# A modulation product moved to plain f32 products on four column groups of TensorE, with its weights in a buffer of their own

## What is computed

```python
silu_c = jax.nn.silu(c)            # 1024 values, the latent stream
silu_cc = jax.nn.silu(c_ctx)       # 1024 values, the context stream
for i in range(DEPTH):             # DEPTH = 2
    m_lat = jnp.split(silu_c @ w_mod[i] + b_mod[i], 9, axis=-1)
    m_ctx = jnp.split(silu_cc @ w_mod[i] + b_mod[i], 9, axis=-1)

def moe_swiglu(h, router, wg, wu, wd):      # first block, second layer
    ...
    for e in range(8):
        out = out + combine[:, e:e + 1] * ((silu(t @ wg[e]) * (t @ wu[e])) @ wd[e])
```

## Time and profile before

| | |
|---|---|
| three executions, median (lowest to highest) | 3621.58 us (3621.06 to 3627.07) |
| the profiled execution | 3618.0 us, span on the core 3616.2 us |
| mean granted TensorE clock | 0.952 |
| TensorE busy with products | 3361.4 us, 93% |
| VectorE / ScalarE / GpSimd busy | 2069.9 / 1639.2 / 492.5 us |
| HBM read | 531.8 MB, 150 GB/s over the span |

### The profile page before, as it was taken

One profiled execution on the slowest core, in us unless ns is written; L12 is line 12 of the kernel. 1 busy time (PEld: TensorE's weight loads), 2 busy tenths in 40 slices (PEclk: granted clock), 3 DMA queues, 4 the chain that ended last, 5 costly groups with the idle time before them and its releaser, 6 DMA issues.

```text
span 3616.2 us, 60330 instructions
## 1 busy us (share of the span) xinstructions
PE 3361.4 (93%) x23090; PEld 3082.0 (85%) x23090; DVE 2069.9 (57%) x3212; ACT 1639.2 (45%) x2673; POOL 492.5 (14%) x558
## 2 busy tenths in 40 slices
PE   7889997779999999998999999989999999988898
PEld 7679997679999999998888897689888988975798
DVE  6855559546666667766333663566336733565554
ACT  4335443345665555655322454544224522344544
POOL 4400007400000000001000241233002400130000
PEclk9779998689999999999999999999999999988999
DMA  5313444326676666764232452134324422340253
GB/s 213 124 49 144 176 157 147 98 103 235 248 253 236 235 240 242 254 243 160 83 110 83 143 184 73 55 117 154 109 82 158 173 101 94 121 152 1 94 186 106
DMA packets 99259, 536.72 MB, mean 148 GB/s; under 512 B 16162, under 2 KB 28002, under 8 KB 51339
## 3 DMA queue, kind: packets, MB, share of 16 engines
q1 hardware_dynamic: 93840, 522.05, 40.8%
q0 software_dynamic: 3200, 9.41, 1.0%
q10 hardware_dynamic: 1978, 1.75, 0.2%
HBM read 531.79 MB, written 10.74 MB: 150 GB/s over the span
## 4 chain that ended last, share of the span: by engine, by line
PE 84%; DVE 9%; ACT 4%; issue 2%; POOL 1%; DMA 0%; ACTq 0%; SPq 0%; DVEq 0%; POOLq 0%
PE PS L966 24%; PE PS L968 23%; PE PS L967 23%; PE PS L1006 4%; PE PS L1133 3%; DVE WL L1597 3%; DVE CONV L1782 3%; PE PS L1112 2%; PE PS L1122 1%; ACT WH L1271 1%; PE PS L1087 1%; POOL TMP L887 1%; DVE RSTD L1614 0%; PE PS L1152 0%; DVE TMP L1916 0%
## 5 line engine op out<-in xcount | busy, mean ns | idle before, releaser
L1597 DVE TENSOR_TENSOR WL<-RAW,WH 128x1024 fp32r<-128x1024 f32 (+2 forms) x1080 | 1228.1, 1142 | 819.0 <-ACT WH L1271 810.9
L966 PE MATMUL PS<-UH,WH 128*128 128x256 f32 (+2 forms) x4672 | 1437.8, 308 | 109.1 <-DVE H L1929 27.1
L1271 ACT ACTIVATE WH<-RAW 128x1024 fp32r<-128x1024 f32 (+2 forms) x1080 | 1049.5, 974 | 960.9 <-PE PS L968 919.7
L967 PE MATMUL PS<-UL,WH 128*128 128x256 f32 (+2 forms) x4672 | 1435.7, 307 | 0.0
L968 PE MATMUL PS<-UH,WL 128*128 128x256 f32 (+2 forms) x4672 | 1433.4, 307 | 0.0
L966 PEld LDWEIGHTS PS<-UH,WH 128*128 128x128 f32 x4672 | 898.6, 192 | 158.1 <-issue 110.7
L968 PEld LDWEIGHTS PS<-UH,WL 128*128 128x128 f32 x4672 | 899.3, 192 | 36.8
L967 PEld LDWEIGHTS PS<-UL,WH 128*128 128x128 f32 x4672 | 896.4, 192 | 38.3
L966 PE MATMUL PS<-HIDH,WH 128*128 128x256 f32 (+2 forms) x1848 | 546.3, 296 | 0.0
L968 PE MATMUL PS<-HIDH,WL 128*128 128x256 f32 (+2 forms) x1848 | 545.2, 295 | 0.0
L967 PE MATMUL PS<-HIDL,WH 128*128 128x256 f32 (+2 forms) x1848 | 545.1, 295 | 0.0
(11 more groups left out here) (184 smaller groups left out, 3030.7 us busy)
## 6 DMA issues: line engine op xcount, KB each, us to landing
RAW<-in_w_gu SPq DMA_DIRECT2D x214, 1024.0 KB, 4.8
RAW<-in_w_dn SPq DMA_DIRECT2D x168, 704.0 KB, 4.1
RAW<-in_w_mod SPq DMA_DIRECT2D x72, 1024.0 KB, 4.9
RAW<-in_w_in SPq DMA_DIRECT2D x30, 1024.0 KB, 5.0
RAW<-in_w_na SPq DMA_DIRECT2D x20, 1024.0 KB, 4.8
RAW<-in_w_o SPq DMA_DIRECT2D x12, 1024.0 KB, 4.8
RAW<-in_w_proj SPq DMA_DIRECT2D x8, 1024.0 KB, 4.8
RAW<-in_w_out SPq DMA_DIRECT2D x8, 1024.0 KB, 4.8
```

Source lines behind the costliest of these rows:

```text
L966: pe.matmul(ps, wh, mh, start=opens and x == 0, stop=False)
L967: pe.matmul(ps, wh, ml, start=False, stop=False)
L1271: act.activation(WH[slot][:, 0:hi - lo], RAW[:, s % RAW_SLOTS, lo:hi], ACT.Copy).then_inc(s_hi, 1)
L1597: dve.tensor_tensor(WL[slot][:, 0:hi - lo], RAW[:, s % RAW_SLOTS, lo:hi], WH[slot][:, 0:hi - lo].bitcast(F32), ALU.subtract).then_inc(s_lo, 1)
```

## The change

- The modulation steps leave the phase "moe": its body now has 19 steps (11 + 8), all evacuated by DVE. `RAW`, `WH` and `WL` see no modulation tile any more, and `SC4` and the work that made it are gone.
- POOL, in a loop of its own, loads each tile of `w_mod` in two halves of 0.5 MB into `MRAW[:, b, :]` (two halves, one transfer each, 144 in all). The transfer for a half is issued when PE has finished the half two before it (`s_mpc`).
- PE does one half after each of the first 18 steps of an expert (`mod_half`): four plain f32 products, with the two conditioning columns `SCF` as the fixed operand (2 columns wide) and 256 moving columns of `MRAW`. Product g writes PSUM partitions 32g and 32g+1, that is column group g of the array, and takes the row chunk 4b+g. The four groups hold four partial sums; two halves (b = 0, 1) accumulate. 72 tiles x 2 halves x 4 = 576 products. PE waits for the weights (`s_mw`) and, at b = 0, for the bank (`s_mev`).
- To leave banks 1 and 3 free for these sums, gate and up of a moe step now share one bank, 256 columns each.
- ACT copies the bank (128 x 256) to `MROW` and sends the four groups with four small transfers (`mod_out`); it does so in every second step, for the tile finished before it. The last tile of an expert (k = 8) is sent at the last step, and the loop's end waits for its landing.
- `mod_rows` and `MLD` are twice as large; behind the loop there are 16 transposes and 16 DVE additions in place of 8 and 8.

```diff
-            add("moe", N_EXP, moe_kinds + "d" * 8, moe_cols + down)
+            add("moe", N_EXP, "d" * 19, full + down)
...
-            SC4 = sb("SC4", [P, KC, 32, 4], F32R, region)
-            MROW = sb("MROW", [4, 2, 256], where=region)
+            MROW = sb("MROW", [P, 2, 256], where=region)
+            MRAW = sb("MRAW", [P, 2, W_STEP // 2], where=region)
...
+            pool.memset(FREE[:, 0:1], 0.0).then_inc(s_mpc, 2)
+            pool.memset(FREE[:, 1:2], 0.0).then_inc(s_mev, 2)
...
+            pool.wait_ge(s_pc, ph["moe"].p0)
+            with pool.Fori(0, N_EXP) as i:
+                for k in range(MOD_PER_EXPERT):
+                    for b in range(2):
+                        pool.wait_ge(s_mpc, i * (2 * MOD_PER_EXPERT) + 2 * k + b + 1)
+                        pool.dma_start(MRAW[:, b, :], ins["w_mod"][i * MOD_PER_EXPERT + k][:, b * 1024:(b + 1) * 1024])\
+                            .then_inc(s_mw[b], 16)
...
-                    for x in range(4):
-                        for w in (WH, WL):
-                            last = pe.matmul(PS[2 * (s % BANK_SETS)][:, 0:256], SC4[:, 4 * h + x, :, :].rearrange("p a b -> p (a b)"),
-                                             w[slot][:, x * 256:(x + 1) * 256], start=(h == 0 and x == 0 and w is WH),
-                                             stop=(h == 1 and x == 3 and w is WL))
+            def mod_half(i, s):
+                k, b = divmod(s, 2)
+                if b == 0:
+                    pe.wait_ge(s_mev, i * MOD_PER_EXPERT + max(k + 1, 2))
+                pe.wait_ge(s_mw[b], (i * MOD_PER_EXPERT + k + 1) * 16)
+                for g in range(4):
+                    last = pe.matmul(PS[1 + 2 * (k % 2)][32 * g:32 * g + 2, 0:256], SCF[:, 4 * b + g, :],
+                                     MRAW[:, b, g * 256:(g + 1) * 256], start=b == 0, stop=b == 1)
+                last.then_inc(s_mpc, 1)
...
+            def mod_out(i, k):
+                act.wait_ge(s_mpc, i * (2 * MOD_PER_EXPERT) + 2 * k + 4)
+                if k >= 2:
+                    act.wait_ge(s_mr[k % 2], (i * len(range(k % 2, MOD_PER_EXPERT, 2)) + k // 2) * 64)
+                act.activation(MROW[:, k % 2, :], PS[1 + 2 * (k % 2)][:, 0:256], ACT.Copy).then_inc(s_mev, 1)
+                act.wait_ge(s_mev, i * MOD_PER_EXPERT + k + 3)
+                for g in range(4):
+                    act.dma_start(mod_rows[g, :, i * MOD_PER_EXPERT + k, :], MROW[32 * g:32 * g + 2, k % 2, :])\
+                        .then_inc(s_mr[k % 2], 16)
...
+                    for g in range(4):
+                        for st in range(2):
+                            for j in range(2):
+                                turned = PS[2 + 2 * (g // 2) + j][:, (2 * (g % 2) + st) * MOD_STEPS:
+                                                                  (2 * (g % 2) + st + 1) * MOD_STEPS]
+                                base = MOD[:, st, :, j] if g else VEC[:, V_BM + j:V_BM + 2 * MOD_STEPS:2]
+                                own.inc(dve.tensor_tensor(MOD[:, st, :, j], turned, base, ALU.add))
+                        dve.wait_ge(s_dve, own.value)
```

More of the change, by code:

```diff
@@ L438, in build @@
         s_mrl = sem("s_mrl")
+        s_mw = [sem(f"s_mw{b}") for b in range(2)]
+        s_mpc = sem("s_mpc")
+        s_mev = sem("s_mev")
         s_mrt = sem("s_mrt")
@@ L648, in pair_banks @@
         def pair_banks(p, s):
[L651 removed]
+            b, n = 2 * (s % BANK_SETS), p.steps[s][3][1] if p.steps else SEQ
             return [PS[b][:, 0:n], PS[b][:, n:2 * n] if n == SEQ else PS[b + 1][:, 0:n]]
@@ L683, in straight, with experts @@
                     load(p, 0, s, w[k0 + s])
-            def experts(name, e0, with_mod=False):
+            def experts(name, e0):
                 p = ph[name]
@@ L728, in _ @@
                 else:
-                    experts("moe", 2, True)
+                    experts("moe", 2)
             def in_steps(name, e0):
@@ L1334, in body @@
                         s += 1
-                        if p.kinds[s] == "a":
-                            ahead(p, i, s, (0,))
-                            multiplied(act, p, i, s)
-                            uses = len(range(k % 2, MOD_PER_EXPERT, 2))
-                            if k >= 2:
-                                act.wait_ge(s_mr[k % 2], (i * uses + k // 2) * 16)
-                            act.activation(MROW[:, k % 2, :], PS[2 * (s % BANK_SETS)][0:4, 0:256], ACT.Copy).then_inc(s_eva, 1)
-                            act.wait_ge(s_eva, p.evacs("a", i, s + 1))
-                            act.dma_start(mod_rows[:, i * MOD_PER_EXPERT + k, :], MROW[:, k % 2, :]).then_inc(s_mr[k % 2], 16)
-                            ahead(p, i, s, (1,))
-                            s += 1
+                        if name == "moe" and k % 2 == 0 and k:
+                            mod_out(i, k // 2 - 1)
                     for m in range(KC):
                         ahead(p, i, s)
+                        if name == "moe" and s % 2 == 0:
+                            mod_out(i, s // 2 - 1)
                         s += 1
-                    if "a" in p.kinds:
+                    if name == "moe":
                         for b in range(2):
-                            act.wait_ge(s_mr[b], (i + 1) * 16 * len(range(b, MOD_PER_EXPERT, 2)))
+                            act.wait_ge(s_mr[b], (i + 1) * 64 * len(range(b, MOD_PER_EXPERT, 2)))
                 iterate(act, p, body)
@@ L1480, in _ @@
                     act.activation(GT[:, :, 1:2], GT[:, :, 0:1], ACT.Exp).then_inc(s_gexp, 1)
-                    act.wait_ge(s_silc, 1)
-                    for k in range(KC):
-                        last = act.activation(SC4[:, k, :, 0:2], SCF[:, k:k + 1, :].to_broadcast([P, 32, 2]), ACT.Copy)
-                    last.then_inc(s_silc, 1)
                     act.wait_ge(s_cbp, 1)
@@ L1867, in _ @@
                     last.then_inc(s_gate, 1)
-                    dve.wait_ge(s_silc, 2)
-                    for k in range(KC):
-                        last = dve.tensor_tensor(SC4[:, k, :, 2:4], SCF[:, k:k + 1, :].to_broadcast([P, 32, 2]),
-                                                 SC4[:, k, :, 0:2].bitcast(F32), ALU.subtract)
-                    last.then_inc(s_silc, 1)
                     dve.wait_ge(s_cb, 4)
```

60 lines of the change are left out of this document (18 added, 42 removed).

## The result

The changed kernel takes 3648.05 us (median of four, 3646.84 to 3656.54) against 3622.60 (four runs of the kernel before beside it): a ratio of 1.0073, 95% interval 1.0055 to 1.0091. It is slower, by 25 us, where 3663 had been forecast. The profiled execution took 3647.39 us with a span of 3645.7, 29.5 more than before. So the time came out near the forecast, but few of the terms that made it up did.

The account below looks back on a forecast made before the run. The prediction took the experts to be bound by TensorE alone. Its terms, -135.4 + 156.2 + 14.4 + 6.6, gave +41.8 us: 3659.8 for the profiled execution, 3663 us as median, range 3560 to 3765.

Parts of the forecast that it names:

- removed, 72 x 1.88: TensorE in the experts: 72 modulation steps of 16 products, 1.88 us each, leave the chain, -135.4 us.
- products of the halves: 144 halves on TensorE: only neighbouring groups overlap, five record places of 0.217 us, 1.085 us a half, +156.2 us; chance 0.36.
- into the narrow shape and out: Changing to the 2-column product shape and back on TensorE: 0.1 us a half, +14.4 us; bounds zero and 0.33 a half.
- turns of the loop: TensorE's seven expert turns: the 19-step shape's 0.85 us wait hides in the 1.9 us PE already stands, so nothing.
- half clock behind them: TensorE's clock falling to its lower level inside the experts: named only as a sign of being wrong, with no price.
- late weights: MRAW loads through POOL: expected hidden, at nothing; the rival had PE wait in down steps, 84 us added, 3654 us, chance 0.08.
- behind the loop: Once after the experts: mod_rows load issued 5.1 us later, twice the data 0.5, eight more transposes 1.0, together +6.6 us.
- side-by-side rival: All four column groups of a half run beside each other, 0.434 + 0.1 us a half: -51.9, 3570 us, chance 0.33.
- its own sign (a half under 0.89 us): Stated test on TensorE's halves: the prediction is wrong if a half takes less than 0.89 us, the point where it gains.
- the two others: Further stated signs of being wrong: TensorE's clock falls to its lower level inside the experts, or a wait for s_mw appears.
- the upper bound of 0.33: Most a half could pay for shape changes: each way costs a product's whole tail, 0.28 less 0.11 us between starts.

Follow-up runs that it names:

- e3: The changed kernel with all eight products of a tile on column group 0, the other three groups' sums left out: 3820.13 us.
- e10: The changed kernel, in its loop, with only one of the four products of each half left (column group 0): 3651.76 us, ratio 1.0079.
- e4: The changed kernel with 96 satisfied waits ahead of TensorE's experts' loop and both halves of a tile multiplied in one visit: 3643.10 us.
- e5: The changed kernel with the experts' loop written out eight times on TensorE, VectorE, ScalarE and SyncE: 3616.25 us, ratio 0.9989.
- e8: e5 with both halves of a tile multiplied together behind the even steps and ScalarE's copy one step behind: 3601.61 us, ratio 0.9944.
- e9: e8 with ScalarE's last tile copied and stored ahead of the next stage's conversions, and mod_rows loaded one step before the last product: 3597.73 us.
- e12: e9 without the 8-byte tile FREE, and with UH and UL moved to 20 bytes beyond a multiple of 64: 3597.91 us, ratio 0.9931.

## Why the forecast was near and its reasons were not

Against the terms, in us of the profiled execution:

```
term                                  forecast   measured
removed, 72 x 1.88                      -135.4     -135.4
products of the halves                  +156.2      +62.5   144 x 0.434
into the narrow shape and out            +14.4      +44.1   144 x 0.306
turns of the loop                          0        +17.9
half clock behind them                     0        +9     at most 12; what is left of the stage's +9.6
late weights                               0         +1.6
spacing of the HIDH/HIDL products     not seen      +18     10 in the experts, 2 ahead, 6 behind
behind the loop                           +6.6      +11.1   last product to the next stage's first
not assigned                               -         +0.5   +2 ahead of the experts, -1.5 in the later stages
sum                                      +41.8      about +29.5
```

*Removed:* right. Before's steps lay in the chain, and the halves that replace them are timed against the same neighbours.

*The four groups:* wrong, and it was the step on which most hung: 1.085 us of stream a half in place of 0.434, 94 us too many. I argued that a record can't start ahead of one that stands before it in the program, so that the second record of a group, which waits for its first, holds up the next group. The trace has four records within 20 ns and then four more; the side-by-side rival, at 0.33, was what happens. All rows I used were of products on one group, and the order of starts there says nothing on groups. The Trainium skill (TensorEngine Tiling (Array Packing), Key Properties) says that tiles do loads and products in parallel; the traces agree (0.235 us for eight records on four groups, 1.51 on one), and I had weighed a general rule on order above it. By its own sign (a half under 0.89 us) the prediction is wrong here, and so it is by the two others: the clock fell inside the experts, and waits for `s_mw` appeared.

*In and out:* the term was right, its size off by three: 0.31 us and not 0.1, just under the upper bound of 0.33 that I took from the tail of a product on each of the two ways. I had chosen by the nearest row, one at half clock between two other shapes. The bound that had a reason behind it, the tail of a product, deserved more weight. e3, e10 and e4 show that it is paid once a visit, whatever is done in it, and the full-width products of L1041 that it is the narrow shape that costs. That it is a drain fits, and isn't shown as such.

*Turns:* "PE already stands 1.9 us, longer than that: nothing". The 0.85 us for the 19-step shape were read rightly (e5 shows 0.9 a turn when the jump is gone), and hiding them behind the jump was right too. What failed was taking the jump's own 1.9 us for a constant. It holds a transfer, and the same change put others ahead of it. The page called that wait "issue" before and a `WL` after; neither names a DMA.

*Clock:* I had named it as a way to be wrong and put no price on it. Behind gaps of 4.3 to 5.0 us it was at the lower level every time, behind those of 1.9 to 2.3 once in seven, behind those of 2.7 to 3.9 (e3) four times in seven. Its 9 us are a remainder and not a measurement; no run separates them from the turns.

*Late weights:* nearly right (1.6 us of waits in place of none), though landings range from 3.3 to 9.7 us with a median of 4.2, my 3.8. Where a buffer is freed later, they don't: 11.1 to 14.6 us in e4, e8, e9 and e12.

*Behind the loop:* the order of events was right, its prices low. The load is issued 7.6 us later and not 5.1; it takes 6.1 us, not 3.8, and ScalarE does two conversions ahead of the last tile's copy, which wait for PE's last products. I had counted one.

*Place:* not seen at all. The diff shows a tile of 8 bytes ahead of two large buffers, and I read it as free.

The side-by-side rival had the right mechanism and the wrong price, 3570 us. Errors of some 64 us too many (groups against the way in and out) and some 51 too few (turns, clock, place, behind the loop) nearly cancelled. That the time came out near the forecast is luck; only the removed part, and the direction that followed from a wrong sum, stand.

## What to carry to other kernels

Small products with few fixed columns are worth packing on column groups: four side by side stream in the time of one (0.43 us here). But each visit costs 0.31 us on top, so collect them. In this loop the jump waited for a transfer of instructions, and that one came behind the data: look at what is on the DMA engines at the jump, or write the loop out (-17 us for before by one line; the best form of the change, e9, is only 5 us better than that). And when a kernel changes, compare the distance of starts of products that were not changed; a new tile ahead of old ones can move them.

## What was not expected of the hardware

The loop of "ffn" has 1734 instructions on TensorE, counted in the program (the trace records 1656 of them), and brings none in its second pass. Kernel before, DMA queues from 380 to 488 us, and kernel after from 908 to 1015 us, one pass of the experts (packets, MB, share):

```profile
q1 hardware_dynamic: 3009, 19.38, 50.0%
q14 instruction: 1, 0.01, 0.0%
```

```profile
q8 instruction: 9, 0.15, 0.6%
```

The jump there takes 0.24 us; in before and after (2068 instructions in after) it takes 3.3 to 6.5 us, and with 1852 (e10) 5.7 to 6.6. The Trainium skill (Runtime: NRT & Kernel Launch, Instruction fetch mechanics) gives TensorE room for 2048 instructions, fetched in blocks of 256, and says that a jump out of the window forces a fetch. The blocks and the forced fetch agree with the traces (16 KB a packet). What the runs show is that 1734 stay and 1852 don't. That needn't contradict the 2048: by the page's blocks of 256, an estimate, 1852 instructions lie in eight or nine blocks and 1734 in seven or eight, and nine packets a pass in e10 fit eight blocks and one fetched ahead. No run here tells.

The address of an operand sets the pace of products on it: 0.1134, 0.1170 or 0.1182 us for the same 128x256 product at the same clock, with `HIDH` at byte 140372 (before), 140436 (e12) or 140380 (after) of the partition, added up from the buffers of each kernel. With 512 columns there is no difference (0.2333 in before and after).
